# Delta rule on one core: state times k subtracted from the scaled values ahead of the block inverse

## What is computed

```
a   = strict_lower((beta k) @ k.T * decay)
sol = triangular_solve(a + I, [beta v, beta k exp(g)])
u, w = sol
step: v_new = u - w @ s
      o     = (q exp(g)) @ s + (lower(q @ k.T * decay)) @ v_new
      s     = s * exp(g_last) + (k exp(g_last - g)).T @ v_new
```

## Time and profile before

| | before |
|---|---|
| median of three runs | 1789.5 us (1789.15 to 1793.75) |
| profiled execution | 1788.49 us |
| span of its trace | 1786.8 us |
| mean granted clock of PE | 0.88 |
| busy PE, DVE, ACT, POOL | 1485.5, 705.6, 405.6, 121.7 us |

### The profile page before, as it was taken

One profiled execution on the slowest core, in us unless ns is written; L12 is line 12 of the kernel. 1 busy time (PEld: TensorE's weight loads), 2 busy tenths in 40 slices (PEclk: granted clock), 3 DMA queues, 4 the chain that ended last, 5 costly groups with the idle time before them and its releaser, 6 DMA issues.

```text
span 1786.8 us, 26537 instructions
## 1 busy us (share of the span) xinstructions
PE 1485.5 (83%) x11278; PEld 1161.9 (65%) x11278; DVE 705.6 (39%) x1206; ACT 405.6 (23%) x559; POOL 121.7 (7%) x162
## 2 busy tenths in 40 slices
PE   3899999985888797972999957998999954999854
PEld 2577777764777653752877836776877743788644
DVE  1667775126554034135111146869711141111106
ACT  2355542112232001021111122362200140110102
POOL 0011111000000040002000020000000002000011
PEclk9899999986888556985999968999999966999986
DMA  6555557600000622113799942003012205999833
GB/s 257 228 230 221 220 221 318 277 1 2 2 3 2 200 71 71 48 47 129 271 353 362 328 171 107 1 0 124 22 54 71 71 0 200 346 352 354 303 141 120
DMA packets 66354, 281.42 MB, mean 158 GB/s; under 512 B 7248, under 2 KB 23888, under 8 KB 42576
## 3 DMA queue, kind: packets, MB, share of 16 engines
q1 hardware_dynamic: 60720, 260.08, 39.0%
q0 software_dynamic: 5536, 19.93, 3.2%
HBM read 228.24 MB, written 51.74 MB: 157 GB/s over the span
## 4 chain that ended last, share of the span: by engine, by line
PE 50%; DVE 8%; ACT 3%; issue 3%; DMA 2%; POOL 1%; SPq 0%; POOLq 0%; DVEq 0%; ACTq 0%
PE acc L643 14%; PE acc L958 14%; PE acc L966 7%; PE acc L1088 2%; PE acc L896 2%; PE acc L876 2%; PE acc L663 1%; PE acc L1054 1%; ACT hT L1215 1%; POOL xs L2309 1%; DMA yT<-xs 1%; PE acc L654 1%; PE acc L1165 1%; DVE rb L1592 1%; DVE zT L2043 1%
## 5 line engine op out<-in xcount | busy, mean ns | idle before, releaser
L643 PE MATMUL acc<-hT,ring 128*128 128x288 f32 x1792 | 444.6, 410 | 13.9 <-ACT hT L1215 11.7
L643 PEld LDWEIGHTS acc<-hT,ring 128*128 128x128 f32 x1792 | 340.8, 191 | 124.5 <-issue 17.7
L958 PEld LDWEIGHTS acc<-zT,ring 128*128 128x128 f32 x2176 | 254.2, 196 | 20.2 <-issue 14.3
L958 PE MATMUL acc<-zT,ring 128*128 128x128 f32 x2176 | 255.0, 279 | 4.6 <-ACT zT L1245 2.3
L966 PE MATMUL acc<-ring,zT 128*128 128x512 f32 x272 | 124.9, 602 | 8.6 <-DVE zT L2043 2.9
L2043 DVE TENSOR_TENSOR zT<-zT,acc 128x256 f32<-128x256 f32 x32 | 13.5, 421 | 240.0 <-ACT zT L1250 240.0
L966 PEld LDWEIGHTS acc<-ring,zT 128*128 128x128 f32 x272 | 48.9, 189 | 64.4 <-issue 62.2
L2048 DVE COPY yT<-acc 128x1024 f32<-128x1024 f32 x32 | 39.2, 1225 | 124.8 <-PE acc L966 124.8
L1250 ACT ACTIVATE zT<-acc 128x256 f32<-128x256 f32 x32 | 12.3, 386 | 316.9 <-PE acc L958 316.9
L949 PE MATMUL acc<-cst,yT 128*128 128x128 f32 x272 | 37.1, 282 | 54.5 <-DMA yT<-xs 54.5
L949 PEld LDWEIGHTS acc<-cst,yT 128*128 128x128 f32 x272 | 32.1, 146 | 56.0 <-issue 53.2
(11 more groups left out here) (434 smaller groups left out, 1944.8 us busy)
## 6 DMA issues: line engine op xcount, KB each, us to landing
ring<-in_w SPq DMA_DIRECT2D x102, 1024.0 KB, 7.8
ring<-in_w_mod_mix SPq DMA_DIRECT2D x24, 1024.0 KB, 8.7
ring<-in_w_mod_ffn SPq DMA_DIRECT2D x24, 1024.0 KB, 7.8
yT<-xs SPq DMA_DIRECT2D x34, 512.0 KB, 8.5
ring<-in_w_in SPq DMA_DIRECT2D x16, 1024.0 KB, 10.7
ys<-yT SPq DMA_DIRECT2D x32, 512.0 KB, 8.0
xs<-S SPq DMA_DIRECT2D x3, 4096.0 KB, 32.6
ring<-in_glu SPq DMA_DIRECT2D x8, 1024.0 KB, 8.5
```

Source lines behind the costliest of these rows:

```text
L643: mm = pe.matmul(ps[:, b, 0:HT], w[:, k, :], rhs[:, k, HT * b:HT * b + HT], start=(k == 0), stop=(k == KD - 1))
L958: mm = pe.matmul(acc[:, H_ACC, x, P * f:P * (f + 1)], wv[:, f, k, :], xt[:, k, :], start=(k == 0), stop=(k == KD - 1), skip_group_check=True)
```

## The change

- The set wT is left out for tiles 0 to 3, and with it ACT's copy of it; tile 4 keeps both. vn of tiles 0 to 3 has only the inverse by VB. It waits for R's copy, for `assemble` and for the new sum on DVE.
- For tiles 1 to 3 a new set ks (k by S) is issued behind X5 of its own tile. DVE multiplies it with the column that was used for KBGT and writes it to KBGT's buffer (`rest_of_state`, in front of KDECT), and adds that to VB (`rest_of_values`, behind `first_inverse`). Tile 0 has a zero state and needs neither. DVE no longer makes KBGT from kt, but for tile 4.
- PE's order inside a tile becomes X1, vn, Q1, gr, X2, o, Q2, su, X3, br, Q3, kk, X4, qk, Q4, kt, X5, ks, Q5, vt, X6, R.
- ACT takes the exponential of gr (now `row_factors`) in front of X2's copy, and DVE gives a semaphore for it after `decay_difference`.
- DVE does step 2 (the product with kk) in front of update 4.

```diff
--- before.py
+++ after.py
@@ -787,27 +787,23 @@
 
             def state_w(t):
                 n = tiles[t][2]
-                if t < 4:
-                    pe.wait_ge(act_drained, at(f"read:R{t}"))
                 pe.wait_ge(inv_assembled, at(f"asm{t}"))
                 pe.wait_ge(dve_drained, at(f"read:kt{t}"))
                 pe.wait_ge(dve_drained, at(f"read:vt{t}"))
                 heads(f"wT{t}", lambda h: ur(KBGT, t, n)[:, h, :], lambda h: um(MT, t, n)[:, h, :],
                       flatbuf(f"wT{t}", H, n))
 
+            def state_k(t):
+                _, c0, n = tiles[t]
+                pe.wait_ge(dve_drained, at(f"S{t - 1}"))
+                heads(f"ks{t}", lambda h: qkv[:, 8 + h, c0:c0 + n], lambda h: S[:, h, :], flatbuf(f"ks{t}", H, P))
+
             def state_v(t):
-                n = tiles[t][2]
-                pe.wait_ge(act_drained, at(f"read:wT{t}"))
-                if t:
-                    pe.wait_ge(dve_drained, at(f"S{t - 1}"))
-                begin(f"vn{t}")
-                out = flatbuf(f"vn{t}", H, P)
-                for h in range(H):
-                    pe.matmul(out[:, h, :], um(MT, t, n)[:, h, :], ur(VB, t, n)[:, h, :], start=True, stop=False,
-                              skip_group_check=True)
-                    mm = pe.matmul(out[:, h, :], um(EX, t, n, P)[:, h, :], S[:, h, :], start=False, stop=True,
-                                   skip_group_check=True)
-                mm.then_inc(acc_full, 1)
+                pe.wait_ge(act_drained, at(f"read:R{t}"))
+                pe.wait_ge(inv_assembled, at(f"asm{t}"))
+                pe.wait_ge(dve_drained, at(f"rest{t}" if t else "read:vt0"))
+                heads(f"vn{t}", lambda h: um(MT, t, P)[:, h, :], lambda h: ur(VB, t, P)[:, h, :],
+                      flatbuf(f"vn{t}", H, P))
 
             def state_o(t):
                 _, c0, n = tiles[t]
@@ -829,32 +825,31 @@
 
             def delta_tile(t):
 
-                if t:
-                    state_w(t - 1)
                 inverse_x(t, 1)
                 if t:
                     state_v(t - 1)
                 inverse_q(t, 1)
-                inverse_x(t, 2)
                 if t < 4:
                     prepare(t + 1, 0)
-                inverse_q(t, 2)
+                inverse_x(t, 2)
                 if t:
                     state_o(t - 1)
-                if t < 4:
-                    inverse_x(t, 3)
+                inverse_q(t, 2)
                 if t:
                     state_s(t - 1)
                 if t == 4:
                     return
+                inverse_x(t, 3)
+                prepare(t + 1, 1)
                 inverse_q(t, 3)
-                prepare(t + 1, 1)
+                prepare(t + 1, 2)
                 inverse_x(t, 4)
-                prepare(t + 1, 2)
+                prepare(t + 1, 3)
                 inverse_q(t, 4)
-                prepare(t + 1, 3)
+                prepare(t + 1, 4)
                 inverse_x(t, 5)
-                prepare(t + 1, 4)
+                if t:
+                    state_k(t)
                 inverse_q(t, 5)
                 prepare(t + 1, 5)
                 inverse_last_x(t)
@@ -1368,17 +1363,21 @@
             act.activation(gt[:, CKDEC], gt[:, G2], ACT.Exp).then_inc(decay_cols_ready, up(decay_cols_ready, "ecol"))
             act.wait_ge(decay_cols_ready, now(decay_cols_ready))
 
+            def row_factors(t):
+                n = tiles[t][2]
+                act.wait_ge(decay_diff_ready, at(f"sub{t}"))
+                if t >= 2:
+                    act.wait_ge(q_decayed, at(f"qdT{t - 2}"))
+                act.activation(um(EG, t, n, P), flatbuf(f"gr{t}", H, n), ACT.Exp).then_inc(
+                    act_drained, up(act_drained, f"read:gr{t}"))
+                act.wait_ge(act_drained, now(act_drained))
+
             def decay_rows(t):
                 n = tiles[t][2]
                 act.wait_ge(decay_diff_ready, at(f"diff{t}"))
                 act.activation(um(EX, t, n), um(EX, t, n), ACT.Exp).then_inc(
                     decay_exp_ready, up(decay_exp_ready, f"ex{t}"))
-                if t >= 2:
-                    act.wait_ge(q_decayed, at(f"qdT{t - 2}"))
-                act.activation(um(EG, t, n, P), flatbuf(f"gr{t}", H, n), ACT.Exp).then_inc(
-                    act_drained, up(act_drained, f"read:gr{t}"))
                 act.wait_ge(decay_exp_ready, now(decay_exp_ready))
-                act.wait_ge(act_drained, now(act_drained))
 
             def pack_a(t):
 
@@ -1428,17 +1427,18 @@
                     act_drained, up(act_drained, f"read:wT{t}"))
                 act.wait_ge(act_drained, now(act_drained))
 
+            row_factors(0)
             decay_rows(0)
             pack_a(0)
             for t, c0, n in tiles:
-                if t:
-                    w_out(t - 1)
                 x_out(t, 1)
                 if t:
                     act.wait_ge(acc_full, filled(f"vn{t - 1}"))
                     act.activation(ur(VN, t - 1, P), flatbuf(f"vn{t - 1}", H, P), ACT.Copy).then_inc(
                         act_drained, up(act_drained, f"read:vn{t - 1}"))
                     act.wait_ge(act_drained, now(act_drained))
+                if t < 4:
+                    row_factors(t + 1)
                 x_out(t, 2)
                 if t < 4:
                     decay_rows(t + 1)
@@ -1775,7 +1775,9 @@
 
                 n = tiles[t][2]
                 dve.wait_ge(acc_full, filled(f"gr{t}"))
-                step(tt(um(EX, t, n), flatbuf(f"gr{t}", H, n)[0:n], bc(gt[0:n, GCOL, t, :], 2, n), ALU.subtract))
+                tt(um(EX, t, n), flatbuf(f"gr{t}", H, n)[0:n], bc(gt[0:n, GCOL, t, :], 2, n), ALU.subtract).then_inc(
+                    decay_diff_ready, up(decay_diff_ready, f"sub{t}"))
+                dve.wait_ge(decay_diff_ready, now(decay_diff_ready))
 
             def prepare(t, step_):
                 _, c0, n = tiles[t]
@@ -1812,7 +1814,9 @@
                         dve.wait_ge(q_decayed, now(q_decayed))
                 elif step_ == 4:
                     dve.wait_ge(acc_full, filled(f"kt{t}"))
-                    start(tt(ur(KBGT, t, n), flatbuf(f"kt{t}", H, P)[0:n], bc(gt[0:n, CKBG, t, :], 2, P), ALU.mult))
+                    if t == 4:
+                        start(tt(ur(KBGT, t, n), flatbuf(f"kt{t}", H, P)[0:n], bc(gt[0:n, CKBG, t, :], 2, P),
+                                 ALU.mult))
                     tt(ur(KDECT, t, n), flatbuf(f"kt{t}", H, P)[0:n], bc(gt[0:n, CKDEC, t, :], 2, P),
                        ALU.mult).then_inc(dve_drained, up(dve_drained, f"read:kt{t}"))
                     dve.wait_ge(dve_order, now(dve_order))
@@ -1822,6 +1826,19 @@
                     tt(ur(VB, t, n), flatbuf(f"vt{t}", H, P)[0:n], bc(gt[0:n, BETA, t, :], 2, P), ALU.mult).then_inc(
                         dve_drained, up(dve_drained, f"read:vt{t}"))
                     dve.wait_ge(dve_drained, now(dve_drained))
+
+            def rest_of_state(t):
+
+                dve.wait_ge(acc_full, filled(f"ks{t}"))
+                tt(ur(KBGT, t, P), flatbuf(f"ks{t}", H, P), bc(gt[:, CKBG, t, :], 2, P), ALU.mult).then_inc(
+                    dve_drained, up(dve_drained, f"read:ks{t}"))
+                dve.wait_ge(dve_drained, now(dve_drained))
+
+            def rest_of_values(t):
+
+                tt(ur(VB, t, P), ur(VB, t, P), ur(KBGT, t, P), ALU.add).then_inc(
+                    dve_drained, up(dve_drained, f"rest{t}"))
+                dve.wait_ge(dve_drained, now(dve_drained))
 
             def first_inverse(t):
 
@@ -1897,12 +1914,16 @@
                     dve.wait_ge(dve_drained, now(dve_drained))
                 if t < 4:
                     prepare(t + 1, 1)
+                    prepare(t + 1, 2)
                     update(t, 4)
-                    prepare(t + 1, 2)
                     prepare(t + 1, 3)
+                    if t:
+                        rest_of_state(t)
                     prepare(t + 1, 4)
                     update_blocks(t)
                     first_inverse(t + 1)
+                    if t:
+                        rest_of_values(t)
                     prepare(t + 1, 5)
             t, _, n = tiles[4]
             for h in range(H):
```

## The result

The changed kernel takes 1779.8 us (median of 6 runs, 1775.6 to 1783.1) beside 1790.4 us for the kernel before in the same series (6 runs). The ratio is 0.9934, with a 95% interval from 0.9923 to 0.9945: by the ratio it is faster by 11.8 us (9.8 to 13.8); the two medians are 10.6 apart. The profiled execution shown here took 1778.05 us, its span 1776.4.

The account below looks back on a forecast made before the run. The delta stage was taken as a chain passing between engines, its waits being the time. Tile 0 -2.0, tiles 1 to 3 +2.3 and tail -7.0 sum to -6.7 us: 1782.8 from 1789.5, range 1777.0 to 1789.0.

Parts of the forecast that it names:

- Head of a tile: Last block product to Q1: without wT, Q1 comes at +8.4 us, a gain of 5.6; DVE's new sum is covered.
- rival C: At vn: it waits behind rest_of_values, tiles 1 to 3 lose 0.9 us more each; 1786.6 us in all, chance 0.26.
- Middle: Q1 to Q3: 13.7 us for 11.59, +2.1, as o's copy queued behind decay_rows delays br.
- End: Q3 to update_blocks: +2.4 us for the order, and +2.0 for kk and X4 after the clock's fall.
- Tiles 1 to 3: The three tiles together: +2.3 us with the clock's fall at kk, -3.3 without it.
- rival D: From kk to ks of tiles 1 to 3: clock stays at 0.50, +3.7 us a tile, 1793.9 us, chance 0.09.
- Tail: Last block product to o3's end: 17.3 us for 24.29, a gain of 7.0.
- Tile 0: First tile: KBGT products fall away and DVE waits less, -2.0 us (0 to -2.4).
- Sum and link: Whole stage: -6.7 us, passed on in full, since PE resumes some 17 us behind o3's end.
- Rival B: At kk: the clock holds, tiles 1 to 3 give -3.3 us; 1777.2 us in all, chance 0.13.

Follow-up runs that it names:

- o3 late: Changed kernel with five extra products of 512 columns, which nobody reads, ahead of o3 alone; ratio 0.9972 to the kernel before.
- new middle, old end: Changed kernel with its new order from X1 to Q2 and Q3 behind br, but the order of before at the tile's end; ratio 0.9923 to the kernel before.
- Holding the clock: Changed kernel with three extra products of 512 columns, which nobody reads, between Q3 and kk in tiles 1 to 3; ratio 0.9941 to the kernel before.
- The removal alone: Changed kernel's algebra, without wT, in the order of the kernel before on PE, ACT and DVE; 1771.4 us, ratio 0.9886 to the kernel before.
- o's copy first: Changed kernel with ACT's copy of o ahead of decay_rows in every tile; ratio 0.996 to the kernel before.

## Why the prediction was right, and where it was not

Forecast: 1782.8 us, 6.7 below the median, faster with the largest chance. Measured: 11.8 below by the ratio. The median is 1779.8, 3.0 below the forecast. Direction and range (1777.0 to 1789.0) hold; the size was short.

- **Head of a tile.** Q1 at +8.4 was forecast; 8.16 in tile 1, 9.26 in tiles 2 and 3, where vn took 3.78, not 3.1, since the clock was still low. rest_of_values cost nothing in the two profiles of the changed kernel, as forecast: no row of vn waits for DVE. But the cover was not the one forecast: vn came right behind X1, since R and X1 ran at half clock. In tile 2 of "o3 late", whose code is the changed kernel's up to there, X6 and R ran at full clock (1.14 each), and vn waited 1.43 for the product with beta, rival C's sign; in tile 2 of "new middle, old end", where the clock fell only under R, it waited 0.72.
- **Middle.** +2.1 forecast, +2.19 in tile 1. The cause named, o's copy behind decay_rows, is shown for 1.0 of it by moving the copy; the rest stays with the new order.
- **End.** +2.4 and +2.0 for the clock forecast; +3.88 in tile 1, and 5.07 in tile 2 (19.49 for 14.42). Holding the clock splits tile 1 into +2.45 for the order and +1.43 for the clock.
- **Tiles 1 to 3.** The mis-sized term: +2.3 forecast, +4.7 measured. The step was "A tile is then -5.6 + 2.1 + 2.4 + 2.0 = +0.9 us": tile 1 is +0.2, tile 2 is +3.25, and tile 3 +1.23 for +0.5. I gave tile 2 the clock of tile 1. Its head stood at 0.50 until past 490.5, through vn and into Q1, which came 0.9 later than forecast; Q1 to Q3 took 0.7 more. Its fall at kk lasted from 508.0 until past 514.5, through X4 and into qk, another 0.7. The last is a part of rival D. It came in the other tiles too: qk took 2.76 and 2.63 in tiles 1 and 2 for 2.05, and in tile 3 the clock was at 0.50 from 549.0 to 555.7, through all of qk. ks ran at full clock each time (2.02), so D did not come whole.
- **Tail.** -7.0 forecast, -8.7 measured. The forecast took o3's end, 17.3, from 24.29; from the whole length, 24.57, it is -7.3. The removal alone gives -6.7; I had no term for the order, which moves o3 ahead of Q2 and gives 2.0 more on top.
- **Tile 0.** -2.0 forecast, -1.6 measured.
- **Sum and link.** Stage -5.7 (199.28 to 193.61) for -6.7: the tiles and the tail were wrong by 2.4 and 1.7 with opposite sign, so that the sum came near by luck. PE resumes 17.2 us behind o3, as forecast.
- **Rival B.** "Tiles 1 to 3 give -3.3" with the clock held. Held in fact, they give +0.2: in tile 1 the head gained 4.8 for 5.6 and the middle lost 2.5 for 2.1, both ahead of the extra products, with the head at half clock. And the tail lost 3.0 against the changed kernel's. B treated the clock as a price at one place; it is not.
- **What no step had.** By the ratio the time fell some 6 us more than the stage did. The stretch behind o3 that the change does not touch differs by up to 7.8 us from one profile to another, and the stage's start by 2.9 (388.06 to 391.00), so single profiles cannot place it; for the removal in the old order stage and ratio agree (19.1 and 20.4 us). So that the time fell more than forecast while the stage fell less is not explained by any step. Whether part of it belongs to the kernel was tried once, with o3 late, and stays open.

The Trainium skill, TensorE: Matmul & The Clock Gate, section "A second HAM failure mode: psum-queue depth-cycling", tells of a kernel whose short pauses between groups of matmuls made the clock swing and cost throughput. The runs agree that it swings between 1.00 and 0.50 here. By that rule the prediction put the time at D's, 11.1 us above the forecast; the run that held the clock prices the falls at kk at 5.6 us in all, near the 2.0 a tile of the forecast. kk waited for su's accumulator before the change too; what the change moved is what stands between Q3 and kk.

## What to carry to other kernels

Leaving work out of a chain and dealing out the rest anew are two changes: time each alone. Here the first was worth 1.1%, and the second gave back about half of it: all of it and more in the loop, though it helped at the end. When an order is written out by hand, look at which set inherits which accumulator: by `begin` the fourth set behind su waits for S whichever set it is. Here that is kk in every order, and it starts 4.33 us behind Q3 in tiles 1 and 2 before and after the change; what the order decides is what PE does until then, and what stands behind kk and is late with it. With br and X4 ahead of kk the pause was 0.99, with neither 3.59.

## What the runs showed of the hardware that I had not expected

The clock does not follow the length of the pause just ahead: after the same 1.76 us it was 1.00 in one tile and 0.50 in the next, and after the same 3.59 us kk of tile 1 took 2.46 and 3.78 in two executions of the changed kernel and 3.79 with o's copy first. And time won at one place was lost at another: with two edits that shortened tiles 1 to 3 by 4.5 and 3.6 us the tail was longer, by 3.0 and 2.7, and the clock stayed at 0.50 for 20.3 us or more, up to 1.0 and 1.2 us ahead of o3's end, for 13.6 in the changed kernel. Each is one profile, so that the edits caused it is likely but not shown. Where the falls lie also moves with one and the same code: Q1 of tile 1 comes 8.16 us behind the last block product in both profiles of the changed kernel and 9.26 in "o3 late", which differs from it only in the tail.
